# A recurrent layer's products and recurrence, in another order

## Chip, core and metric

The kernel runs on one core of a Trainium2 chip. The metric is the time of one execution on the device in microseconds (us). PE is TensorE, DVE is VectorE, ACT is ScalarE, POOL is GpSimd, SP is SyncE, which issues the loads of weights.

## What is computed

Four layers over 512 tokens of width 1024, all in float32: dilated attention with a SwiGLU FFN, forgetting attention with a SwiGLU FFN and a last norm, then a second block of a gated recurrent mixer and a retention mixer, each between an input norm and an output norm. The change is in the recurrent mixer:

```python
u = h @ w_in                                  # 1024 -> 2 x 1536
xb, gate = u[..., :D_RNN], u[..., D_RNN:]
xb = causal_depthwise_conv(xb, conv_w, conv_b)         # 4 taps
xblk = xb.reshape(bsz, s, 16, 96)
r = sigmoid(einsum('bsnc,ncd->bsnd', xblk, w_a) + b_a)
i = sigmoid(einsum('bsnc,ncd->bsnd', xblk, w_x) + b_x)
log_a = -8.0 * r * softplus(-lam)
a = exp(log_a)
bt = sqrt(-expm1(2.0 * log_a)) * (i * xb)
hseq = associative_scan over tokens: h[t] = a[t] * h[t-1] + bt[t]
y = hseq * silu(gate)
return y @ w_out                              # 1536 -> 1024
```

Its input is the first block's output: the last norm of the first block and the input norm of the mixer are folded into one.

## The kernel before

Activations lie with the feature in the partition and the 512 tokens along the row: a tile is 128 x 512. The residual R has 8 such tiles, a projection's input is a pair XH, XL (a value rounded to fp32r, and what is left of it), and each product is three matmuls: high by high, high by low, low by high. Weights come in units of 128 x 1024 (512 KB) in the order of the program through a ring of 5 slots (RING). SP loads unit u when unit u - 5 is used; ACT makes WH of it (L1053), DVE makes WL (L1561). On both, `split(end)` does this for all units up to `end`, where it stands in the engine's program. A unit of a projection is 24 matmuls of 512 columns (L525): two k by four output tiles by three. PSUM has 8 banks; a group of 4 units fills four of them.

Every engine runs its program in order, with semaphores between them. The order is written out by hand.

Ahead of the recurrent layer stands the second FFN's down projection (D1, 22 units). Its second half ends with four additions to R (`add_out`, L1595), and behind them stand ACT's eight XH (L1251) and DVE's eight XL (L1969). POOL sums squares of R in two ways (L1513 to L1520, `two_norms` on PE multiplies the sums by ones) for the folded norms. DVE then makes the factor RB in three steps (`rb_var`, L1975 to L1979), ACT its root, DVE the reciprocal.

The layer (U["L"], 24 units): three times a group of 4 units for the convolution's input (banks 0 to 3) and a group of 4 for the gate (banks 4 to 7). After a first group DVE scales four tiles into L_XR (L2021), ACT makes the last tap (L1268), DVE the three others (L2008), ACT the high part CH (L1272), DVE the low part CL (L2013). After a second group DVE scales four tiles into L_G (L2032), ACT takes their sigmoid (L1279), POOL multiplies (L1523). Behind the first group DVE also runs `after_first_inputs`: R is scaled with the last norm of the first block (L1985, L1989), and `softplus` of lam in 18 small steps.

Then the block products (U["LG"], 8 units, L961 to L963): for each of four blocks of 3 tiles, one unit for r and one for i, 21 matmuls each. A block's round behind them: six sigmoids (ACT, L1295), exp and tanh (ACT, L1307, L1312), CH + CL, i * x and a * a (POOL, L1532, L1536, L1538), the energy (DVE, L2059), its root (ACT, L1300), i times it (DVE, L2040), three scans (DVE, L2043), the product with the gate (DVE, L2047), high and low of the outputs into CH and CL (ACT L1319, DVE L2053). The products of block j wait for the sigmoids of block j - 1, and those of blocks 2 and up stand on ACT behind the outputs of block j - 2. Last the output projection (U["LO"], 12 units: two groups of 6), sums of squares (L976), and the output norm.

## Time and profile before

| | us |
|---|---|
| median of three runs | 2365.08 (2364.07 to 2365.3) |
| the profiled execution | 2365.22 |
| its span, first to last instruction | 2363.4 |
| PE busy in the span | 2238.7 (95%) |
| DVE, ACT, POOL busy | 1225.6, 798.2, 536.0 |

Times of rows are microseconds from the span's start. A timeline row gives start, busy time, engine, line, operation and tiles; in brackets the idle time before it and what ended that. Rows with x3 hold three instructions. Matmuls overlap, so a row's 0.39 is longer than the distance of two starts.

### The profile page before, as it was taken

The page shows a single profiled execution, that of the slowest core. Times are in us where ns is not written, and L with a number is a line of the kernel's source. Part 1 is how long each engine was busy: PE and PEld are TensorE (multiplying, and loading weights), DVE is VectorE, ACT ScalarE, POOL GpSimd, SP SyncE. Part 2 cuts the span into 40 slices and gives each one's busy share as a digit, 9 for nine tenths or more (in the row PEclk, how much of TensorE's full clock was granted, in tenths as well). Part 3 has the DMA queues.
Part 4 walks back from the last instruction along what each step waited for, and adds up shares of the span by engine and source line. Part 5 has one row for each costly group of instructions (what it writes and reads, how often), then busy time and mean ns, then how long its engine had stood idle before and what let it go on. Part 6 is the DMA issues. An engine that isn't in the chain of part 4 may idle for free.

```text
span 2363.4 us, 26705 instructions
## 1 busy us (share of the span) xinstructions
PE 2238.7 (95%) x10598; PEld 1797.5 (76%) x10598; DVE 1225.6 (52%) x1987; ACT 798.2 (34%) x1334; POOL 536.0 (23%) x355
## 2 busy tenths in 40 slices
PE   7999999998999999999999999998994879999997
PEld 6788886886788888876668888887773757877876
DVE  4666456565644433455457444326848665443342
ACT  3334332443332222233434222213346423323321
POOL 2443234140501101223324011034025131100100
PEclk9999999999999999999999999999997999999999
DMA  4222221221233333332213333332321213222322
GB/s 140 81 68 76 81 81 58 68 72 54 81 98 98 96 94 97 98 99 81 72 63 98 96 93 96 99 98 74 96 89 54 72 59 97 85 76 76 93 77 72
DMA packets 84155, 198.27 MB, mean 84 GB/s; under 512 B 7216, under 2 KB 44208, under 8 KB 84032
## 3 DMA queue, kind: packets, MB, share of 16 engines
q1 hardware_dynamic: 81408, 189.62, 26.2%
q10 hardware_dynamic: 2624, 6.93, 0.9%
q8 instruction: 86, 1.41, 0.3%
q14 instruction: 37, 0.30, 0.0%
HBM read 194.40 MB, written 2.13 MB: 83 GB/s over the span
## 4 chain that ended last, share of the span: by engine, by line
PE 85%; DVE 9%; ACT 3%; issue 2%; DMA 0%; POOL 0%; DVEq 0%; SPq 0%; ACTq 0%
PE PS L525 50%; PE PS L569 5%; PE PS L571 5%; PE PS L570 5%; PE PS L594 2%; PE PS L595 2%; PE PS L596 2%; PE PS L1018 1%; PE PS L642 1%; PE PS L652 1%; PE PS L666 1%; DVE WL L1561 1%; PE PS L897 1%; PE PS L887 1%; ACT WH L1053 1%
## 5 line engine op out<-in xcount | busy, mean ns | idle before, releaser
L1561 DVE TENSOR_TENSOR WL<-WR,WH 128x1024 fp32r<-128x1024 f32 x353 | 478.3, 1365 | 759.0 <-ACT WH L1053 758.3
L1053 ACT ACTIVATE WH<-WR 128x1024 fp32r<-128x1024 f32 x353 | 369.6, 1056 | 709.8 <-DMA WR<-in_ws 700.5
L525 PE MATMUL PS<-XH,WH 128*128 128x512 f32 x1024 | 404.8, 395 | 20.4 <-ACT XH L1062 12.0
L525 PE MATMUL PS<-XH,WL 128*128 128x512 f32 x1024 | 401.5, 392 | 0.0
L525 PE MATMUL PS<-XL,WH 128*128 128x512 f32 x1024 | 401.3, 392 | 0.0
L525 PEld LDWEIGHTS PS<-XH,WH 128*128 128x128 f32 x1024 | 194.1, 190 | 66.1 <-issue 21.1
L569 PE MATMUL PS<-XH,WH 128*128 128x512 f32 x544 | 225.1, 414 | 5.4 <-DVE WL L1561 3.6
L525 PEld LDWEIGHTS PS<-XL,WH 128*128 128x128 f32 x1024 | 194.1, 190 | 41.1 <-issue 1.2
L525 PEld LDWEIGHTS PS<-XH,WL 128*128 128x128 f32 x1024 | 193.9, 189 | 40.9
L571 PE MATMUL PS<-XH,WL 128*128 128x512 f32 x544 | 215.8, 397 | 0.0
L570 PE MATMUL PS<-XL,WH 128*128 128x512 f32 x544 | 215.1, 395 | 0.0
L1451 POOL TENSOR_TENSOR A_SH<-A_SH,A_SIN 128x512 f32<-128x512 f32 x48 | 82.5, 1720 | 270.8 <-DVE A_SH L1746 270.8
L1473 POOL TENSOR_TENSOR F_U<-F_G,F_U 128x1024 f32<-128x1024 f32 x22 | 52.7, 2394 | 400.0 <-DVE F_G L1826 400.0
L525 PE MATMUL PS<-HH,WL 128*128 128x512 f32 x352 | 137.0, 389 | 0.0
L525 PE MATMUL PS<-HL,WH 128*128 128x512 f32 x352 | 137.0, 389 | 0.0
L525 PE MATMUL PS<-HH,WH 128*128 128x512 f32 x352 | 137.0, 389 | 0.0
L569 PEld LDWEIGHTS PS<-XH,WH 128*128 128x128 f32 x544 | 104.5, 192 | 28.1 <-issue 5.0
L1083 ACT ACTIVATE A_P<-A_P,A_ST 128x128 f32<-128x128 f32 (+1 forms) x192 | 79.7, 417 | 131.9 <-DVE A_ST L1689 131.9
L571 PEld LDWEIGHTS PS<-XH,WL 128*128 128x128 f32 x544 | 103.9, 191 | 23.5
L570 PEld LDWEIGHTS PS<-XL,WH 128*128 128x128 f32 x544 | 104.6, 192 | 19.1
L525 PE MATMUL PS<-WH,XH 128*128 128x512 f32 x256 | 99.7, 390 | 0.0
L525 PE MATMUL PS<-WL,XH 128*128 128x512 f32 x256 | 99.7, 389 | 0.0
(332 smaller groups left out, 3763.1 us busy)
## 6 DMA issues: line engine op xcount, KB each, us to landing
WR<-in_ws SPq DMA_DIRECT2D x281, 512.0 KB, 3.6
WR<-in_ws SPq DMA_DIRECT2D x144, 256.0 KB, 3.1
B_CB<-gates ACTq DMA_DIRECT2D x8, 512.0 KB, 3.9
XTOK<-in_x SPq DMA_DIRECT2D x2, 1024.0 KB, 8.4
out<-OUT SPq DMA_DIRECT2D x4, 512.0 KB, 2.6
R_D<-in_decay ACTq DMA_DIRECT2D x4, 256.0 KB, 2.6
GAIN<-in_post ACTq DMA_DIRECT2D x1, 512.0 KB, 5.0
CST<-in_cst SPq DMA_DIRECT2D x1, 320.0 KB, 3.3
```

The costliest lines, as they stand in the source:

```text
L525: mm = pe.matmul(PS[:, bank + o, :], l, r, start=first and kk == 0 and i == 0, stop=last and kk == 1 and i == 2)
L569: pe.matmul(PS[:, bank + o, :], WH[:, s, cols], hi[:, k, :], start=first, stop=False)
L570: pe.matmul(PS[:, bank + o, :], WH[:, s, cols], lo[:, k, :], start=False, stop=False)
L571: return pe.matmul(PS[:, bank + o, :], WL[:, s, cols], hi[:, k, :], start=False, stop=last)
L594: pe.matmul(PS[:, o, :], xh, wh, start=first and kk == 0, stop=False)
L595: pe.matmul(PS[:, o, :], xh, wl, start=False, stop=False)
L596: mm = pe.matmul(PS[:, o, :], xl, wh, start=False, stop=last and kk == 1)
L1053: nc.scalar.activation(WH[:, s, :], WR[:, s, :], ACT.Copy).then_inc(hi_ready, 1)
L1083: x = nc.scalar.activation(A_P[:, n % 2, h, w], A_P[:, n % 2, h, w], ACT.Exp, bias=stat(m, 0, 2 * pair + h, qb), accum_out=stat(m, 1, 2 * ...
L1451: nc.gpsimd.tensor_tensor(A_SH[:, r % 2, :], A_SH[:, r % 2, :], A_SIN[:, :], ALU.mult).then_inc(rot_m, 1)
L1473: nc.gpsimd.tensor_tensor(F_U[:, :, :], F_G[:, :, :], F_U[:, :, :], ALU.mult).then_inc(ht_ready, 1)
L1561: tt(WL[:, s, :], WR[:, s, :], WH[:, s, :].bitcast(F32), ALU.subtract).then_inc(lo_ready, 1)
```

## The change

The weights' order in the layer is a table now, L_ORDER: all 12 units of the convolution's input first, then block 0, the first gate group, block 1, half of the second gate group, block 2, its other half, block 3, the third gate group. PE follows it. The convolution's buffers L_XR and L_XC hold four tiles, L_G holds four tiles instead of twelve, so the gate product and the outputs go in fours (`out_inputs`, `out_sigmoids`, `out_gates`, `outputs`). Block products use banks 4 to 7 in rotation: the first tile of each group is given back earlier, and from the fifth tile on (q = 4) a product waits for a sigmoid of the same block. The groups of the output projection change banks. The new helpers hold the same operations as the loops before: `last_tap` and `conv_high` (ACT) and `convolve` and `conv_low` (DVE) for a convolution tile; `gate_sigmoids`, `decays` (exp and tanh), `energy_root`, and `recurrent_high` (ACT), `energy`, `recur` (product and three scans), `outputs` and `outputs_lows` (DVE), and `recur` on POOL (CH + CL, i * x, a * a) for a block's round. On ACT the last four convolution tiles are begun with L_XR of the third group, so they and all before them stand ahead of the first `gate_sigmoids`. `softplus` stands after the second four convolution tiles. The scaling of R moves behind the recurrence (`first_output`), and the four first XL lows into the down projection's second half.

```diff
+        L_ORDER = [("x", j, i) for j in range(3) for i in range(4)] + [("gates", 0, i) for i in range(2)]
+        L_ORDER += [("g", 0, i) for i in range(4)] + [("gates", 1, i) for i in range(2)]
+        L_ORDER += [("g", 1, i) for i in range(2)] + [("gates", 2, i) for i in range(2)]
+        L_ORDER += [("g", 1, i) for i in range(2, 4)] + [("gates", 3, i) for i in range(2)]
+        L_ORDER += [("g", 2, i) for i in range(4)]
...
-            for j in range(3):
-                if j:
-                    pe.wait_ge(xr_ready, 4 * j)
-                group(U["L"] + 8 * j, 4, XH, XL, 0, ready=x_ready(6),
-                      between=None if j else {3: two_norms})
-                pe.wait_ge(rb_var, 6)
-                if j:
-                    pe.wait_ge(lg_ready, 4 * j)
-                group(U["L"] + 8 * j + 4, 4, XH, XL, 4)
-            pe.wait_ge(xr_ready, 12)
-            pe.wait_ge(lg_ready, 12)
-            for j in range(4):
+            def first_product(j):
+                def free(o):
+                    if j == 1 and o == 2:
+                        pe.wait_ge(rb_var, 6)
+                    if j == 2 and o == 0:
+                        pe.wait_ge(xr_ready, 4)
+                group(at_l("x", j, 0), 4, XH, XL, 4 * (j % 2), ready=None if j else x_ready(6),
+                      between=None if j else {3: two_norms}, free=free)
+            def gate_product(j, a, b):
+                if a == 0:
+                    if j:
+                        pe.wait_ge(lg_ready, 4 * j)
+                    else:
+                        pe.wait_ge(xr_ready, 12)
+                for i in range(a, b):
+                    unit(at_l("g", j, i), i, XH, XL, 0, i == 0, i == 3, True)
+            def block_products(j):
                 pe.wait_ge(ch_ready, 3 * j + 3)
                 pe.wait_ge(cl_ready, 3 * j + 3)
+                if j:
+                    pe.wait_ge(sig_done, 6 * j)
+                else:
+                    pe.wait_ge(xr_ready, 8)
                 for which in range(2):
-                    u = U["LG"] + 2 * j + which
+                    u = at_l("gates", j, which)
                     s = u % RING
                     pe.wait_ge(lo_ready, u + 1)
-                    if j:
-                        pe.wait_ge(sig_done, 6 * (j - 1) + 3 * which + 3)
                     for o in range(3):
+                        q = 3 * which + o
+                        if q >= 4:
+                            pe.wait_ge(sig_done, 6 * j + q - 3)
                         blocks = [(n, i) for n, (i, oo) in enumerate(GATE_BLOCKS) if oo == o]
                         for n, i in blocks:
                             cols = slice(n * P, (n + 1) * P)
-                            b = PS[:, 4 * which + o, :]
+                            b = PS[:, 4 + q % 4, :]
                             pe.matmul(b, WH[:, s, cols], CH[:, 3 * j + i, :], start=n == blocks[0][0], stop=False)
                             pe.matmul(b, WH[:, s, cols], CL[:, 3 * j + i, :], start=False, stop=False)
                             mm = pe.matmul(b, WL[:, s, cols], CH[:, 3 * j + i, :], start=False,
                                            stop=n == blocks[-1][0])
-                    mm.then_inc(unit_used, 1)
+                        mm.then_inc(unit_used if o == 2 else gate_done, 1)
+            for j in range(3):
+                first_product(j)
+            block_products(0)
+            gate_product(0, 0, 4)
+            block_products(1)
+            gate_product(1, 0, 2)
+            block_products(2)
+            gate_product(1, 2, 4)
+            block_products(3)
+            gate_product(2, 0, 4)
             pe.wait_ge(sig_done, 24)
...
-            group(U["LO"], 6, CH, CL, 0, ready=recurrent)
-            group(U["LO"] + 6, 6, CH, CL, 4, between={3: lambda: post_sums(0, 4)})
+            group(U["LO"], 6, CH, CL, 4, ready=recurrent)
+            pe.wait_ge(lg_ready, 12)
+            group(U["LO"] + 6, 6, CH, CL, 0, between={3: lambda: post_sums(0, 4)})
...
-            split(U["D1"] + 26)
             act.wait_ge(gv_ready, 2)
             for k in range(DT):
+                if k == 4:
+                    split(U["D1"] + 26)
...
+                last_tap(4 * j)
+                last_tap(4 * j + 1)
                 for o in range(4):
...
+                    split(u + min(4 * j + 9 + o, 18))
+                    conv_high(4 * j + o)
+                    if o < 2:
+                        last_tap(4 * j + 2 + o)
+            gate_sigmoids(0)
+            decays(0)
+            split(u + 19)
+            energy_root(0)
+            split(u + 21)
+            out_sigmoids(0)
+            split(u + 22)
+            gate_sigmoids(1)
+            split(u + 24)
+            decays(1)
+            split(u + 25)
+            energy_root(1)
+            split(u + 26)
+            gate_sigmoids(2)
+            split(u + 28)
+            decays(2)
+            split(u + 29)
+            recurrent_high(0)
+            out_sigmoids(1)
+            split(u + 30)
+            energy_root(2)
+            gate_sigmoids(3)
+            split(u + 31)
+            decays(3)
+            split(u + 32)
+            recurrent_high(1)
+            split(u + 33)
+            energy_root(3)
+            split(u + 36)
+            out_sigmoids(2)
+            recurrent_high(2)
...
-                    act.wait_ge(y_done, 4)
+                    act.wait_ge(cl_ready, 2 * LT)
                 for k in range(4 * d, 4 * d + 4):
-                    nc.scalar.activation(L_G[:, k, :], PS[:, k, :], ACT.Square).then_inc(post_sq, 1)
+                    nc.scalar.activation(L_SQ[:, k, :], PS[:, (k + 4) % 8, :], ACT.Square).then_inc(post_sq, 1)
...
+            recur(0)
+            out_gates(0)
+            recur(1)
+            recur(2)
+            out_gates(1)
+            recur(3)
+            out_gates(2)
...
+            def folded_low(k):
+                dve.wait_ge(x_hi, 48 + k + 1)
+                dve.wait_ge(r_done, 32 + k + 1)
+                stt(XL[:, k, :], R[:, k, :], GV[:, 1, k:k + 1], XH[:, k, :].bitcast(F32), ALU.mult, ALU.subtract)\
+                    .then_inc(x_lo, 1)
+            for d in range(2):
+                split(dn + (26 if d else 15))
+                dve.wait_ge(unit_used, dn + 11 * (d + 1))
+                for k in range(4 * d, 4 * d + 4):
+                    r_inc(tt(R[:, k, :], R[:, k, :], PS[:, k, :], ALU.add))
+                    if k % 4:
+                        folded_low(k - 1)
+                folded_low(4 * d + 3)
...
-            for k in range(DT):
-                dve.wait_ge(x_hi, 48 + k + 1)
-                stt(XL[:, k, :], R[:, k, :], GV[:, 1, k:k + 1], XH[:, k, :].bitcast(F32), ALU.mult, ALU.subtract)\
-                    .then_inc(x_lo, 1)
...
+            def out_inputs(j):
+                dve.wait_ge(unit_used, at_l("g", j, 3) + 1)
+                if j:
+                    dve.wait_ge(y_done, j)
+                for o in range(4):
+                    tt(L_G[:, o, :], PS[:, o, :], RB[:, 0:T], ALU.mult).then_inc(lg_ready, 1)
...
+                first_inputs(j)
                 for o in range(4):
...
+                    convolve(c)
+                    split(u + min(9 + c, 18))
...
+                if j == 1:
+                    dve.wait_ge(ls_exp, 1)
+                    softplus()
+            energy(0)
+            split(u + 20)
+            recur(0)
+            split(u + 21)
+            out_inputs(0)
+            split(u + 24)
+            energy(1)
+            split(u + 25)
+            recur(1)
+            split(u + 26)
+            outputs(0)
+            split(u + 28)
+            out_inputs(1)
+            split(u + 29)
+            outputs_lows(0)
+            energy(2)
+            split(u + 30)
+            recur(2)
+            split(u + 31)
+            outputs(1)
+            split(u + 32)
+            outputs_lows(1)
+            energy(3)
+            split(u + 34)
+            recur(3)
+            split(u + 36)
+            out_inputs(2)
+            outputs(2)
+            outputs_lows(2)
+            first_output()
```

ACT's program between the convolution and the first decays. L_XC is the convolution's sum, CH its high part, WH a unit's high part, L_G the gate, L_SG its sigmoid, L_R and L_I the two sigmoids of a block. Before:

```order
L1268 ACTIVATE L_XC<-L_XR,VC 128x512
L1272 ACTIVATE CH<-L_XC 128x512
L1053 ACTIVATE WH<-WR 128x1024 x4
L1279 ACTIVATE L_SG<-L_G 128x512 x4
L1295 ACTIVATE L_R<-PS,VC 128x512 x3
L1295 ACTIVATE L_I<-PS,VC 128x512 x3
L1053 ACTIVATE WH<-WR 128x1024 x2
L1307 ACT_TABLE_LOAD
L1307 ACTIVATE L_A<-L_R,L_S 128x512 x3
L1312 ACTIVATE L_R<-L_R,L_S 128x512 x3
L1295 ACT_TABLE_LOAD
L1295 ACTIVATE L_RB<-PS,VC 128x512 x3
```

and now:

```order
L1308 ACTIVATE L_XC<-L_XR,VC 128x512 x2
L1095 ACTIVATE WH<-WR 128x1024
L1315 ACTIVATE CH<-L_XC 128x512
L1308 ACTIVATE L_XC<-L_XR,VC 128x512
L1095 ACTIVATE WH<-WR 128x1024
L1315 ACTIVATE CH<-L_XC 128x512
L1308 ACTIVATE L_XC<-L_XR,VC 128x512
L1315 ACTIVATE CH<-L_XC 128x512 x2
L1331 ACT_TABLE_LOAD
L1331 ACTIVATE L_R_117<-PS,VC 128x512 x3
L1331 ACTIVATE L_I_118<-PS,VC 128x512 x3
L1341 ACT_TABLE_LOAD
```

Between the last convolution tile and the sigmoids of block 0 stood four units and a gate group; now the sigmoids follow at once, and units are split between the convolution's tiles.

ACT around the last block. Before, from the outputs of block 1 (L1319) to the decays of block 3:

```order
L1319 ACTIVATE CH<-L_AB 128x512 x3
L1295 ACT_TABLE_LOAD
L1295 ACTIVATE L_RB<-PS,VC 128x512 x3
L1295 ACTIVATE L_IB<-PS,VC 128x512 x3
L1053 ACTIVATE WH<-WR 128x1024 x2
L1300 ACT_TABLE_LOAD
```

and now, from the first four outputs (L1365) to the sigmoids of block 3 (L1331):

```order
L1365 ACTIVATE CH<-L_W 128x512 x4
L1359 ACT_TABLE_LOAD
L1359 ACTIVATE L_SG<-L_G 128x512 x4
L1095 ACTIVATE WH<-WR 128x1024
L1351 ACT_TABLE_LOAD
L1351 ACTIVATE L_W<-L_W 128x1536
L1331 ACT_TABLE_LOAD
L1331 ACTIVATE L_R_122<-PS,VC 128x512 x3
L1331 ACTIVATE L_I_123<-PS,VC 128x512 x3
```

The gate's sigmoids and the root of block 2 now stand ahead of the sigmoids of block 3.

DVE around the scaling of R (L1989 before, L2091 now; WL is a unit's low part). Before, between the last low of the first convolution group and the small steps of softplus:

```order
L2013 TENSOR_TENSOR CL<-L_XC,CH 128x512
L1561 TENSOR_TENSOR WL<-WR,WH 128x1024 x4
L1985 RECIPROCAL L_X<-L_X 128x512
L1989 SCALAR_TENSOR_TENSOR R<-R,VC,L_X 128x512 x8
L1864 TENSOR_SCALAR L_S<-L_S 128x12
```

and now, behind the recurrence, ahead of the output projection's units from the fifth on:

```order
L1654 TENSOR_TENSOR WL<-WR,WH 128x1024 x2
L2133 TENSOR_TENSOR L_G<-PS,RB 128x512 x4
L2157 TENSOR_TENSOR L_W<-L_H,L_G 128x2048
L2163 TENSOR_TENSOR CL<-L_W,CH 128x512 x4
L2087 RECIPROCAL L_X<-L_X 128x512
L2091 SCALAR_TENSOR_TENSOR R<-R,VC,L_X 128x512 x8
L1654 TENSOR_TENSOR WL<-WR,WH 128x1024 x6
```

The reciprocal and the eight products moved behind 24 more units' low parts, and six of the projection's units stand behind them.

## Rows read from the trace of the kernel before

**Rows 1.** The page: PE's busy time, and the weights' loads (KB, us to landing).

```profile
PE 2238.7 (95%) x10598; PEld 1797.5 (76%) x10598; DVE 1225.6 (52%) x1987; ACT 798.2 (34%) x1334; POOL 536.0 (23%) x355
...
WR<-in_ws SPq DMA_DIRECT2D x281, 512.0 KB, 3.6
```

**Rows 2.** Timeline of PE from the down projection's end to the output projection.

```profile
1610.81 0.77 PE L525 MATMUL PS<-XH,WH 128*128 128x512 f32 x1 [4.11 <-DVE XL L1969]
...
1636.34 1.02 PE L935 MATMUL PS<-L_X,CST 128*128 128x512 f32 x2
...
1639.54 0.50 PE L525 MATMUL PS<-XH,WH 128*128 128x512 f32 x1 [2.19 <-DVE RB L1979]
...
1757.11 0.77 PE L961 MATMUL PS<-CH,WH 128*128 128x512 f32 x1 [4.01 <-issue]
...
1780.63 0.77 PE L961 MATMUL PS<-CH,WH 128*128 128x512 f32 x1 [2.81 <-ACT L_RB L1295]
...
1806.81 0.77 PE L961 MATMUL PS<-CH,WH 128*128 128x512 f32 x1 [14.82 <-ACT L_R L1295]
...
1833.52 0.80 PE L525 MATMUL PS<-CH,WH 128*128 128x512 f32 x1 [14.79 <-ACT L_IB L1295]
...
1862.88 0.80 PE L525 MATMUL PS<-CH,WH 128*128 128x512 f32 x1 [4.94 <-DVE WL L1561]
```

**Rows 3.** Chain of waits in the output projection: start, us, what.

```profile
1897.24 3.43 PE PS L976 x8
1900.67 10.91 PE PS L525 x48
```

**Rows 4.** One stretch: us, busy of PE, PEld, DVE, ACT, POOL, PEclk, DMA, GB/s.

```profile
1806.80:1811.20 4.40, 4.39 (x10) 3.46 (x11) 1.82 (x1) 4.38 (x6) 2.65 (x1) 0.50 0.00 0
```

**Rows 5.** Timeline of POOL: norm sums, gate products, recurrence.

```profile
1630.47 2.28 POOL L1520 TENSOR_TENSOR L_X<-L_X 128x512 f32<-128x512 f32 x1
...
1680.17 5.11 POOL L1523 TENSOR_TENSOR L_G<-L_G,L_SG 128x512 f32<-128x512 f32 x4 [47.42 <-ACT L_SG L1279]
...
1790.25 3.28 POOL L1538 TENSOR_TENSOR L_EB<-L_AB 128x1536 f32<-128x1536 f32 x1 [3.21 <-ACT L_AB L1307]
1793.49 4.33 POOL L1532 TENSOR_TENSOR L_X<-CH,CL 128x1536 f32<-128x1536 f32 x1
```

**Rows 6.** Timeline of DVE in the recurrent layer.

```profile
1649.54 2.46 DVE L2008 SCALAR_TENSOR_TENSOR L_XC<-L_XR,VC,L_XC 128x512 f32<-128x512 f32 x3
...
1652.69 0.69 DVE L2013 TENSOR_TENSOR CL<-L_XC,CH 128x512 fp32r<-128x512 f32 x1 [0.70 <-ACT CH L1272]
...
1666.42 3.35 DVE L1985 RECIPROCAL L_X<-L_X 128x512 f32<-128x512 f32 x1
...
1669.80 5.39 DVE L1989 SCALAR_TENSOR_TENSOR R<-R,VC,L_X 128x512 f32<-128x512 f32 x8
...
1678.74 2.48 DVE L2032 TENSOR_TENSOR L_G<-PS,RB 128x512 f32<-128x512 f32 x4
...
1749.98 4.63 DVE L1561 TENSOR_TENSOR WL<-WR,WH 128x1024 fp32r<-128x1024 f32 x4 [0.26 <-ACT WH L1053]
...
1790.96 9.06 DVE L2043 TENSOR_TENSOR_SCAN L_R<-L_A,L_I 128x512 f32<-128x512 f32 x3
...
1829.38 1.75 DVE L2059 SCALAR_TENSOR_TENSOR L_E<-L_E,L_R 128x1536 f32<-128x1536 f32 x1
...
1856.44 3.46 DVE L2043 TENSOR_TENSOR_SCAN L_RB<-L_AB,L_IB 128x512 f32<-128x512 f32 x3
```

**Rows 7.** Timeline of ACT: table load, sigmoids, root, the output norm's root.

```profile
1777.34 1.28 ACT L1295 ACT_TABLE_LOAD   x1
1778.64 1.84 ACT L1295 ACTIVATE L_RB<-PS,VC 128x512 f32<-128x512 f32 x3
...
1785.42 1.49 ACT L1300 ACTIVATE L_E<-L_E 128x1536 f32<-128x1536 f32 x1
...
1916.78 0.63 ACT L1067 ACTIVATE RB<-RB 128x512 f32<-128x512 f32 x1 [3.11 <-DVE RB L1578]
```

264 lines of the change are left out of this document (126 added, 138 removed).

## The prediction

> **What bounds the kernel now.** I read the page's engine line first: PE (TensorE) is busy for 95% of the span, so only its idle places and its slow clock can be won back [rows 1]. Then PE's timeline through the recurrent layer, where the change is, with the idle time and its releaser in brackets [rows 2]. From the last matmul of the second FFN's down projection (1610.81 less 4.11, so 1606.7 us) to the end of the last L525 matmul of the layer's output projection at 1911.6 [rows 3] are 304.9 us. The work there is 24 + 12 units of 24 matmuls and 8 block units of 21: 1032 matmuls at 0.2273 us (10.91 for 48) are 234.6 [rows 3], and the two norm products and four first sums take 5.3 [rows 2, 3]. Some 65 us are left: 47.7 are the seven idle times of [rows 2], the rest is slow clock and small gaps. After an idle time the granted clock is 0.50, the lower of its two levels (1.2 GHz), for some 4 to 5 us (4.4 in the stretch shown) [rows 4]; a matmul then takes 0.43, so each restart costs some 2 us. The two waits of 14.8 us say what bounds the stretch: PE has only block products left and stands until ScalarE's sigmoids, which stand behind the recurrence chain VectorE, ScalarE, GpSimd. One such round is 26.7 us (1806.81 to 1833.52).
>
> Three prices run through the sum. A VectorE op with its inputs in SBUF and a GpSimd op keep each other waiting: three scans take 3.46 alone and 9.06 beside two GpSimd ops, whose ends at 1793.53 and 1797.82 fit the scans' [rows 5, 6]. A change of function set on ScalarE is 1.28, and the next set's first op starts 0.02 behind it [rows 7]. A unit's low half (WL) takes 1.15 (4.63 for four) [rows 6], after landing in 3.6 [rows 1].
>
> **The change, part by part.** I walk the changed order from 1606.7, engine by engine, with these durations.
>
> *Start.* The lows of XL for k 0 to 3 move into the down projection's second half, beside 11 units of 5.45 us in each of which VectorE makes one WL of 1.15, and PE begins at 1606.7 instead of 1610.8. Four units take 21.8: 1628.5. But the norm products wait for GpSimd's sums, which ended at 1632.75 and start from the same residual tiles as before [rows 5]; with four XL ops fewer beside them I take 1631.0. So of 4.1 plus its slow restart only some 4 remain. The norms take 1.9, VectorE's three steps to rb_var 2.2 as before [rows 2] with six matmuls of the next group ahead of the wait. Then 186 matmuls, 42.3: first_product(2) ends at 1677.4.
>
> *Block 0.* PE goes on for 27 matmuls, 6.1. The fourth tile of six (q = 4) reuses bank 4 and waits for the first sigmoid, which on ScalarE stands behind all twelve convolution tiles; the last four of these begin only when first_product(2) has ended. From 1677.4: a WL's rest and two lows, 1.7; softplus, 3.6 (1678.74 less the end of L1989); four L_XR, 2.5 (as the four L_G); four tiles of taps at 2.46, 9.8; two WL, 2.3; two lows, 1.3; CH 0.6; table load 1.28; a sigmoid 0.6 (1.84 for three) [rows 6, 7]. Together 23.7: 1701.0. PE stands 17.5, **a new stall** that replaces the 4.0, 2.8 and one of the 14.8. After it 15 matmuls, 3.4, and 2.4 for slow clock: 1706.8.
>
> *Middle.* Four g units 21.8, block 1 9.5, two g units 10.9, block 2 9.5 and 0.6 of wait, two g units 10.9: 1770.0. Here the g products hide the recurrence: a round's chain of 20 to 27 us lies beside 20.5 to 31 us of matmuls, where before it lay beside 9.5.
>
> *Block 3.* PE needs its sigmoid at 1776.1. On ScalarE sqrt of block 2 stands ahead, on VectorE out_inputs(1) ahead of that, and this waits for the g unit that ends at 1770.0. Chain: 2.8 because the WL of two units stand behind GpSimd's ops of 3.3 us and more; L_G 2.5; WL 1.15; four lows of outputs beside GpSimd's four L_G products (5.11 for four), 4.9; energy for three tiles 1.75; sqrt 1.5; table load 1.3; sigmoid 0.6: 16.5 [rows 5 to 7], so 1786.5, a wait of 10.4. Then 3.4 and 2.4: 1792.3. The last g product, 21.8: 1814.1.
>
> *Output projection.* Its first four units run to 1835.9. The low of the fifth is on VectorE behind first_output, which the change moves there: reciprocal 3.35 and eight R 5.4 [rows 6]. VectorE gets there late: from 1792.3 GpSimd's three ops of a block (3.4 each, 10.2, between 3.28 and the 4.33 of one held up, and 2.4 lost to VectorE's) to 1804.9; WL, four lows and energy 5.4; sqrt and two WH 2.5, with a wait, 3.6 in all; product and three scans 5.2; two WL 2.3; four L_G 2.5; GpSimd's four products from the first sigmoid on, to 1827.8; product 2.3; high and lows 3.1; first_output 8.8; WL 1.15: 1843.1. PE waits 7.2. Then eight units 43.6, first sums 3.4, slow clock 2.4: **1892.5**. first_output was free before, since it ran in the projection's shadow; here it is the whole of this stall.
>
> *Behind it* nothing changes in kind: squares, sums and the output norm are the same ops in other banks. ScalarE needs one more table load before the root, and it waits 3.11 there for rb_var, so the 1.28 is hidden [rows 7]; without that cover it would cost 1.28.
>
> Sum: 1892.5 against 1911.6, a gain of 19.1. The profiled execution took 2365.22 (span 2363.4), within 0.15 of the median; that gives **2346**.
>
> *Table loads, row and rule.* The row shows 1.28 and no gap after it [rows 7]. The Trainium skill, "ScalarE: Activation LUTs", What ACT_TABLE_LOAD costs, gives 2.66 us for each switch, 1.38 of it a drain. By it three switches on PE's path (blocks 0, 3 and the last sigmoids) would make an estimate 4 us later, 2350. The trace does not show the drain.
>
> *The port, row and rule.* By [rows 5, 6] GpSimd and VectorE wait for each other, but not wholly: part of each GpSimd op runs beside. The Trainium skill, "SBUF — State Buffer", SBUF: two separate sides, calls it an exclusive lock for the whole instruction. By that rule each of the pairs above costs some 0.4 more, about 2 us in all, 2348.
>
> **Rivals.**
> 1. *The port costs less.* If in the new order the pairs miss each other (scans at 3.46 as in the fourth block before), the 2.8 and 2.4 in block 3, 2.4 in the next chain and 1 at the start go, and with them half of what the four lows lose, about 10: 2336. For it: ops without a partner run at the solo price in [rows 6]. Against: the order puts GpSimd's L_G products beside the output lows.
> 2. *More waits at the blocks.* Chains through three in-order queues tend to lose a little at each link. If block 2 waits as block 3 does (10.4 less 0.6) and restarts slow (2.4), 12 are lost: 2358; if it waits half as long, 2352. Against: ScalarE's work ahead of block 2's sigmoid is done 0.6 after PE needs it, by the same prices.
> 3. *Slower.* The g products do not hide the rounds: each block's round of 26.7 starts only when the g product before it is done, because out_inputs(j), the WL of the next units and the sigmoids stand in line behind it on VectorE and ScalarE. For it: before, each round did run alone [rows 2]; against: then PE had nothing else to do. Then from 1706.8: three rounds, 80.1, and 65.4 of g products, 1852.3; projection and its waits 78.4: 1930.7, 19.1 later than before: 2384. It decides at overlap: my forecast has 38 of the 65.4 hidden, and below 19 the change is a loss.
> 4. *Block 0's stall is shorter*, if VectorE is not behind with softplus: 3.6 less, 2342; inside the range.
>
> **How the numbers follow.** The walk as it stands 0.62 (2341 to 2351); rival 1 0.15; rival 2 0.16; rival 3 0.04; rival 4 0.03. The range 2336 to 2356 leaves out the end of rival 1, the far end of rival 2 and rival 3. A difference of 0.2% (5 us) is about what a measurement of this kernel can tell. Faster by more 0.93 (all but the far end of rival 2 and rival 3), same 0.03, slower 0.04.
>
> **What would show it.** In PE's timeline after: no wait at the first unit, one of 2 to 4 us before the norm products; one of 17 in block 0 released by a sigmoid; one of 5 to 12 in block 3; one of 3 to 9 at the fifth unit of the output projection, released by WL; the first output matmul at 1814, the last at 1892. The prediction is wrong if block 1 or 2 waits by more than 3 us, if scans take 9 as a rule, or if the norm's tail grows.

## The result and the profile after

| | before | after |
|---|---|---|
| median, us | 2365.19 (2364.07 to 2365.59, four runs) | 2348.28 (2346.45 to 2349.87, four runs) |
| profiled execution, its span | 2365.22, 2363.4 | 2346.45, 2344.7 |
| end of D1 (last down projection matmul) to end of the output projection | 304.9 | 288.9 |
| from there to the end of the span | 451.8 | 451.8 |

After is 0.9929 of before, with a 95% interval of 0.9913 to 0.9945: 16.9 us less. The forecast walked from D1's end on and gave 19.1 less; from there 16.0 were measured. The time of 2348.28 is 2.3 above the forecast and inside its range.

Both spans are cut at D1's end because PE's program ahead of it is the same and still ends at different times: 1606.7 before, 1603.9 after, and between 1603.7 and 1608.2 in the profiled executions below. D1 itself takes 119.8 in every one of them, whether the four XL lows stand in its second half or not, so the difference arises ahead of it. Whoever compares two single spans puts up to 4.6 us of that down to the change.

The page of after, first section. It answers [rows 1]:

```profile
PE 2230.0 (95%) x10598; PEld 1790.5 (76%) x10598; DVE 1214.4 (52%) x1986; ACT 802.6 (34%) x1337; POOL 544.3 (23%) x355
```

PE is busy 8.7 us less with as many matmuls, as these count longer at the lower clock (5.8 of it between D1's end and the output projection's, 255.2 against 249.4), and its share is 95% in both: this line says little of where the gain is. PE's timeline can. These are all its idle times over 1 us from D1's end to the output projection's end, and the one behind (start, us, what, and in brackets the idle time and its releaser). They answer [rows 2]:

```profile
1629.53 1.49 PE L950 MATMUL PS<-SQS,CST 128*128 128x512 f32 x2 [3.85 <-POOL L_X L1605]
...
1700.57 0.80 PE L992 MATMUL PS<-CH,WH 128*128 128x512 f32 x1 [17.09 <-ACT L_R L1331]
...
1755.92 0.50 PE L992 MATMUL PS<-CH,WH 128*128 128x512 f32 x1 [1.20 <-ACT L_R L1331]
...
1786.12 0.80 PE L992 MATMUL PS<-CH,WH 128*128 128x512 f32 x1 [9.50 <-ACT L_R L1331]
...
1842.94 0.79 PE L541 MATMUL PS<-CH,WH 128*128 128x512 f32 x1 [7.50 <-DVE WL L1654]
...
1906.48 0.77 PE L541 MATMUL PS<-XH,WH 128*128 128x512 f32 x1 [9.20 <-ACT XH L1104]
```

Before, there were eight over 1 us, 49.0 in all: the seven of [rows 2] and this one:

```profile
1686.50 0.47 PE L525 MATMUL PS<-XH,WH 128*128 128x512 f32 x1 [1.30 <-DVE WL L1561]
```

Now they are 39.1 in five. So 9.9 of the 16.0 are idle time, and nearly all the rest is the 5.8 of matmuls at the lower clock. The wait at the layer's first unit is gone, so are both of 14.8. 17.09 is new, and the 4.94 at the fifth unit of the output projection has become 7.50. The chain of waits says what bounds the start (start, us, what); here is its end:

```profile
1624.97 2.06 POOL L_X L1600
1627.03 1.22 POOL SQS L1603
1628.25 1.23 POOL L_X L1605
1629.53 1.49 PE PS L950 x2
1631.01 1.72 PE PS L951 x2
```

From 1606.05 to 1629.5 the chain runs on GpSimd, while PE works beside it. Two stretches of the clock (us, busy of PE, PEld, DVE, ACT, POOL, PEclk, DMA, GB/s), the norm products and the restart in block 0, as in [rows 4]:

```profile
1629.50:1632.70 3.20, 3.17 (x5) 1.39 (x6) 0.00 (x0) 0.00 (x0) 0.00 (x0) 0.60 0.00 0
1700.50:1704.90 4.40, 4.33 (x10) 3.50 (x11) 0.00 (x0) 1.83 (x5) 0.00 (x0) 0.50 0.00 0
```

### The profile page after: what moved, and what is told of

It is laid out like the page before. It is cut to its first block, busy times and chain, and to the rows that moved or that the text cites. A ratio compares the mean times of both kernels' runs of the same rounds, so it can differ in the third digit from the quotient of the medians.

```text
span 2344.7 us, 26703 instructions
## 1 busy us (share of the span) xinstructions
PE 2230.0 (95%) x10598; PEld 1790.5 (76%) x10598; DVE 1214.4 (52%) x1986; ACT 802.6 (34%) x1337; POOL 544.3 (23%) x355
## 3 DMA queue, kind: packets, MB, share of 16 engines
q1 hardware_dynamic: 81408, 189.62, 25.6%
## 4 chain that ended last, share of the span: by engine, by line
PE 85%; DVE 8%; issue 2%; ACT 2%; POOL 2%; DMA 1%; DVEq 0%; SPq 0%; POOLq 0%; ACTq 0%
PE PS L541 50%; PE PS L585 5%; PE PS L587 5%; PE PS L586 5%; PE PS L610 2%; PE PS L611 2%; PE PS L612 2%; PE PS L1060 2%; PE PS L658 1%; PE PS L668 1%; PE PS L682 1%; PE PS L913 1%; PE PS L903 1%; DVE WL L1654 1%; ACT WH L1095 1%
## 5 line engine op out<-in xcount | busy, mean ns | idle before, releaser
L541 PE MATMUL PS<-XH,WH 128*128 128x512 f32 x1024 | 403.1, 394 | 13.0 <-ACT XH L1104 12.7
L586 PEld LDWEIGHTS PS<-XL,WH 128*128 128x128 f32 x544 | 103.7, 191 | 19.1
L541 PE MATMUL PS<-WH,XL 128*128 128x512 f32 x256 | 99.6, 389 | 0.0
```

The lines of the kernel that those rows point to most:

```text
L541: mm = pe.matmul(PS[:, bank + o, :], l, r, start=first and kk == 0 and i == 0, stop=last and kk == 1 and i == 2)
L586: pe.matmul(PS[:, bank + o, :], WH[:, s, cols], lo[:, k, :], start=False, stop=False)
```

## The experiments

All were run against the kernel before; the comparison with after goes through that. The intervals are 2 to 4 us to either side, so a difference of less than some 5 us between two medians is not resolved by them. "Rest" is the span less the end of D1 in the profiled execution (740.7 in after, 756.7 before). It leaves out the part ahead of D1's end, but there is one for each kernel. How well it repeats can be seen where the order is the same: from D1's end to the restart in block 0 is 96.7 to 97.4 in five kernels (after, e_first_early, e_pool_short, e_energy_first, e_g_not_split). Smaller differences below go by the rest and by the waits.

| run | median | of before (95%) | rest |
|---|---|---|---|
| e_first_early | 2338.99 | 0.9888 (0.9873 to 0.9903) | 730.4 |
| e_pool_short | 2343.61 | 0.9908 (0.9895 to 0.9922) | 737.1 |
| e_energy_first | 2345.56 | 0.9919 (0.9905 to 0.9933) | 737.5 |
| e_lows_late | 2351.94 | 0.9943 (0.9931 to 0.9956) | 741.9 |
| e_norm_short | 2341.35 | 0.9899 (0.9882 to 0.9915) | 734.3 |
| e_g_not_split | 2359.84 | 0.9979 (0.9971 to 0.9988) | 752.3 |
| e_sig0_early | 2346.18 | 0.9921 (0.9908 to 0.9933) | 737.3 |
| e_block0_chain | 2341.86 | 0.9902 (0.9888 to 0.9915) | 735.1 |
| e_all | 2335.09 | 0.9873 (0.9860 to 0.9887) | 727.4 |
| e_all_pool_order | 2332.53 | 0.9860 (0.9845 to 0.9875) | 725.3 |
| e_best | 2329.69 | 0.9849 (0.9834 to 0.9863) | 719.6 |
| e_best2 | 2327.60 | 0.9839 (0.9826 to 0.9853) | 719.7 |

### Does first_output make the last wait?

```diff
+            first_output()
             energy(0)
...
             outputs_lows(2)
-            first_output()
```

> The changed kernel with one move: first_output (one reciprocal and eight scaled R tiles on VectorE) stands just before the energy of block 0, in VectorE's idle 17.39 us there, and no longer between the output lows and the low half of the projection's fifth unit. Theory A (first_output is the whole of that stall): the wait of 7.50 at the fifth unit of the output projection goes, and with it some 2 us of slow clock: 8 to 10 us less than the changed kernel's 2348.3, so 2338 to 2341; PE's waits in blocks 0, 2 and 3 stay at 17, 1 and 9.5. Rival B (something else is about as late): the low half then waits for the output highs and lows, for its landing or for WH, and only 0 to 4 us are gained, 2344 to 2348. Rival C: the R tiles beside GpSimd's first ops of block 0 hold those up, and block 2's wait grows by what GpSimd loses, 3 us or more.

Theory A: 9.3 less in the medians, 10.3 in the rest. PE has no idle time over 0.3 us in the output projection, and those in blocks 0, 2 and 3 are 17.30, 1.19 and 9.50. Its last two R tiles lie beside GpSimd's first ops now, and VectorE pays most for it (timeline of VectorE, then of GpSimd, in this run):

```profile
1706.10 11.91 DVE L2091 SCALAR_TENSOR_TENSOR R<-R,VC,L_X 128x512 f32<-128x512 f32 x8
1720.73 1.76 DVE L2140 SCALAR_TENSOR_TENSOR L_W<-L_W,L_R 128x1536 f32<-128x1536 f32 x1 [2.72 <-POOL L_W L1624]
```

```profile
1713.61 3.85 POOL L1621 TENSOR_TENSOR L_I<-L_I,L_W 128x1536 f32<-128x1536 f32 x1
1717.54 3.08 POOL L1624 TENSOR_TENSOR L_W<-L_A 128x1536 f32<-128x1536 f32 x1
```

11.91 instead of 5.39 [rows 6], all of it in the last two tiles (4.01 and 4.00, where the six ahead took 0.75 each), while GpSimd's op took 3.85 for 3.52 in after, and VectorE still waits 2.72 for GpSimd behind them. Rivals B and C fall.

### What makes block 3's wait?

Two runs: GpSimd's products of the second group shortened, and, with nothing left out, another order on VectorE.

```diff
-                    nc.gpsimd.tensor_tensor(L_G[:, o, :], L_G[:, o, :], L_SG[:, o, :], ALU.mult).then_inc(lgs_ready, 1)
+                    n = 1 if j == 1 else T
+                    nc.gpsimd.tensor_tensor(L_G[:, o, 0:n], L_G[:, o, 0:n], L_SG[:, o, 0:n], ALU.mult).then_inc(lgs_ready, 1)
```

> The changed kernel in which GpSimd's four L_G products of the second output group cover 1 of 512 columns (the rest of that group's gate product is left out). They lie beside VectorE's four output lows (6.81 us, against 2.49 alone) ahead of block 3's sigmoid. Theory A (block 3's wait is made by these pairs): the lows take 2.5, the energy, the root and the sigmoid come 4 to 4.5 earlier, PE's wait in block 3 falls from 9.50 to 5 to 5.5, and the time by 4 to 5: 2343 to 2344.5. Rival B (the lows are not on that chain, or the root's table load and WH stand there anyway): block 3's wait stays above 8 and the time within 1 of 2348.3. Rival C (later waits take it back): block 3's wait falls but the one at the projection's fifth unit grows, gain under 2.

```diff
-            outputs_lows(0)
             energy(2)
+            outputs_lows(0)
```

> The changed kernel with two steps swapped on VectorE: the energy of block 2 ahead of the four output lows of the first group, not behind them; nothing is left out. Theory A (in the run with GpSimd's L_G products cut to one column PE's wait in block 3 fell from 9.50 to 5.18, so what counts there is the 6.81 us of lows beside them): the energy starts some 6 to 7 earlier, takes 2 to 4 beside GpSimd, and the root follows: PE's wait in block 3 falls to 3.5 to 5.5, 4 to 6 us less than 2348.3: 2342 to 2344.5. Rival B (the energy itself is held up by GpSimd's products, or the lows now hold up VectorE's product and scans and so outputs of group 1): block 3's wait falls but a later wait grows, gain under 2.

The rows of after first: VectorE's four lows, GpSimd's products beside them.

```profile
1774.07 6.81 DVE L2163 TENSOR_TENSOR CL<-L_W,CH 128x512 fp32r<-128x512 f32 x4
1780.80 1.74 DVE L2140 SCALAR_TENSOR_TENSOR L_W<-L_W,L_R 128x1536 f32<-128x1536 f32 x1
```

```profile
1773.00 7.33 POOL L1610 TENSOR_TENSOR L_G<-L_G,L_SG 128x512 f32<-128x512 f32 x4
```

Shortened, they leave the lows alone (VectorE's timeline in e_pool_short):

```profile
1775.42 2.49 DVE L2164 TENSOR_TENSOR CL<-L_W,CH 128x512 fp32r<-128x512 f32 x4
```

and PE a wait of 5.18 instead of 9.50: 4.3 less, 4.7 in the medians, 3.7 in the rest, and the wait at the fifth unit stays at 7.49: theory A, and rivals B and C fall. The new order brings it down further, to 3.88, but 2.62 come up behind it. PE's timeline in e_energy_first, and VectorE's:

```profile
1783.92 0.79 PE L992 MATMUL PS<-CH,WH 128*128 128x512 f32 x1 [3.88 <-ACT L_R L1331]
...
1802.52 0.50 PE L541 MATMUL PS<-XH,WH 128*128 128x512 f32 x1 [2.62 <-DVE WL L1654]
```

```profile
1788.82 10.02 DVE L2149 TENSOR_TENSOR_SCAN L_H<-L_A,L_I 128x512 f32<-128x512 f32 x3
1798.76 3.70 DVE L1654 TENSOR_TENSOR WL<-WR,WH 128x1024 fp32r<-128x1024 f32 x1
```

The scans (3.46 in after) now meet GpSimd's ops of block 3 and take 10.02, with a low half behind them. The wait at the fifth unit falls to 5.79. In sum 2.7 less in the medians and 3.3 in the rest, where A wanted 4 to 6 and B under 2: block 3's wait fell as A said, and a later one took part of it back, as B said.

### What is the start worth?

```diff
-                    if k % 4:
-                        folded_low(k - 1)
-                folded_low(4 * d + 3)
...
+            for k in range(DT):
+                folded_low(k)
```

> The changed kernel with the lows of XL after all eight R adds of the down projection again, as in the kernel before; all else as changed. Theory A (the start is bound by GpSimd's norm sums, so folding the lows is worth little): PE waits some 4 us at the first unit and restarts slowly, but no longer waits before the norm products (3.85 now), which run at full clock: 0.5 to 2.5 us slower than 2348.3, so 2349 to 2351. Rival B (the fold is worth its whole wait): 4 to 6 us slower, 2352 to 2354. Rival C (the sums are slowed by the folded lows as much as these save): the same or up to 2 us faster, 2346 to 2348.

```diff
+                w = 1 if k == 7 else T
-                nc.gpsimd.tensor_tensor(first[:, :], R[:, k, :], R[:, k, :], ALU.mult).then_inc(sq_mul, 1)
+                nc.gpsimd.tensor_tensor(first[:, 0:w], R[:, k, 0:w], R[:, k, 0:w], ALU.mult).then_inc(sq_mul, 1)
```

(and `w` columns in the three steps behind it; the rest of the last tile's part of both sums is left out)

> The changed kernel in which GpSimd's four steps of the norm sums for the last residual tile cover 1 of 512 columns (the rest of that tile's part of both sums is left out). They took 5.6 us, and PE waited 3.85 for the last of them before the norm products. Theory A (the start of the layer is bound by GpSimd's sums, and all that follows hangs on it): no wait before the norm products, which then run at full clock and no longer take 3; every later wait of PE stays as it was; 4.5 to 6.5 us less than 2348.3: 2342 to 2344. Rival B (the next link, from VectorE's steps on the norm to the convolutions, is as late): the wait in block 0 grows by what the start gains; within 2 of 2348.3.

With the lows late PE waits 3.96 at the first unit and not at all before the norms; the restart in block 0 is 98.8 after D1's end instead of 96.7, and 1.2 of that is left in the rest. The medians say 3.7, between theories A and B, and the intervals overlap; the waits and the rest say A, that most of the fold is not gained, since GpSimd's sums come next. The other run shows the other side. PE's timeline in e_norm_short:

```profile
1628.24 1.02 PE L950 MATMUL PS<-SQS,CST 128*128 128x512 f32 x2
1629.10 1.02 PE L951 MATMUL PS<-L_X,CST 128*128 128x512 f32 x2
1629.56 0.79 PE L541 MATMUL PS<-XH,WH 128*128 128x512 f32 x1
...
1698.19 0.80 PE L992 MATMUL PS<-CH,WH 128*128 128x512 f32 x1 [17.31 <-ACT L_R L1331]
```

No wait, 1.32 from the first norm product to the next unit's first matmul (2.20 in after, from 1629.53 to 1631.73), and all behind it 5 us earlier, with the same wait in block 0. 6.9 less in the medians, 6.5 in the rest: theory A, a little above its 4.5 to 6.5. GpSimd's sums were worth more than their wait of 3.85.

### Do the g units hide the rounds?

```diff
-        L_ORDER += [("g", 1, i) for i in range(2)] + [("gates", 2, i) for i in range(2)]
-        L_ORDER += [("g", 1, i) for i in range(2, 4)] + [("gates", 3, i) for i in range(2)]
+        L_ORDER += [("gates", 2, i) for i in range(2)]
+        L_ORDER += [("g", 1, i) for i in range(4)] + [("gates", 3, i) for i in range(2)]
...
-            gate_product(1, 0, 2)
             block_products(2)
-            gate_product(1, 2, 4)
+            gate_product(1, 0, 4)
```

> The changed kernel in which the second gate group of the projection is not split: all four of its units (21.8 us of PE) stand between block 2 and block 3, none between block 1 and block 2. The work is the same. Theory A (a round of the recurrence costs PE what of it is not beside g units): block 2 loses 10.9 of cover, and its wait goes from 1.20 to 10 to 13; block 3's sigmoid waits for the L_G of units that now end some 11 to 13 later, so its wait stays at 8 to 10: 10 to 14 slower than 2348.3, 2358 to 2362. Rival B (the rounds are paced by their own chain, 27 to 30 from sigmoid to sigmoid, wherever the g units stand): block 2 waits 10 more and block 3 10 less, and the time stays within 3 of 2348.3.

PE's timeline:

```profile
1759.27 0.79 PE L992 MATMUL PS<-CH,WH 128*128 128x512 f32 x1 [10.76 <-ACT L_R L1330]
...
1801.13 0.79 PE L992 MATMUL PS<-CH,WH 128*128 128x512 f32 x1 [8.62 <-ACT L_R L1330]
```

Block 2 waits 10.76 instead of 1.20, block 3 8.62 instead of 9.50, and the time grows by 11.6 (and as much in the rest): theory A. With the same work, two units taken from between the rounds cost their own 10.9.

### Is block 0's wait ScalarE's order?

```diff
                     split(u + min(4 * j + 9 + o, 18))
+                    if j == 2 and o == 0:
+                        gate_sigmoids(0, 0, 4)
                     conv_high(4 * j + o)
...
+                    if j == 2 and o == 1:
+                        gate_sigmoids(0, 4, 6)
-            gate_sigmoids(0)
```

> The changed kernel with one move on ScalarE: the first four sigmoids of block 0 stand behind the first low of the third group of convolutions is due (after its first two last taps), the last two after its last tap, no longer all six behind the twelfth convolution tile. Theory A (block 0's 17 us are ScalarE's order alone): the first sigmoid starts at about 13 us earlier, PE's wait in block 0 falls from 17.09 to 3 to 5, ScalarE's decays and so the energy of block 0 come 9 to 12 earlier (VectorE idles there for 5 to 8 rather than 17.39), waits in blocks 2 and 3 grow by 0 to 4 together: 8 to 12 us less than 2348.3, so 2336 to 2340. Rival B (the later chain does not follow): GpSimd's first ops now lie beside VectorE's taps and both lose time, and the later blocks' waits grow by most of what block 0 gave: a gain under 4, 2344 to 2349.

My theory fell on its size: 2.1 in the medians, 3.4 in the rest, for 8 to 12. Block 0's wait did fall to 4.40. But (PE's timeline, then VectorE's, then GpSimd's)

```profile
1690.97 0.50 PE L992 MATMUL PS<-CH,WH 128*128 128x512 f32 x1 [4.40 <-ACT L_R L1333]
...
1731.63 0.80 PE L992 MATMUL PS<-CH,WH 128*128 128x512 f32 x1 [6.96 <-ACT L_R L1333]
```

```profile
1696.59 8.75 DVE L2124 SCALAR_TENSOR_TENSOR L_XC<-L_XR,VC,L_XC 128x512 f32<-128x512 f32 x3
...
1715.24 1.76 DVE L2145 SCALAR_TENSOR_TENSOR L_W<-L_W,L_R 128x1536 f32<-128x1536 f32 x1 [5.54 <-POOL L_W L1629]
```

```profile
1696.40 3.62 POOL L1622 TENSOR_TENSOR L_W<-CH,CL 128x1536 f32<-128x1536 f32 x1 [63.80 <-PE PS L994]
1700.10 3.83 POOL L1626 TENSOR_TENSOR L_I<-L_I,L_W 128x1536 f32<-128x1536 f32 x1
```

The early sigmoids and products let GpSimd start 13 us sooner, beside VectorE's taps, and these took 8.75 instead of 2.46. ScalarE's decays still stood behind the last convolution tile, and this came late by that. So the energy came 4.5 earlier, not 9 to 12 (from D1's end), and block 1, which had not waited, waited 6.96 for a sigmoid that stands behind `out_sigmoids(0)`. The next run moves `decays(0)` behind the last of the early sigmoids, and `gate_sigmoids(1)` ahead of `out_sigmoids(0)`:

```diff
                     if j == 2 and o == 1:
                         gate_sigmoids(0, 4, 6)
+                        decays(0)
-            decays(0)
...
+            gate_sigmoids(1)
             out_sigmoids(0)
...
-            gate_sigmoids(1)
```

> The run with block 0's sigmoids moved gained 2.1 where 8 to 12 were expected: its trace shows three taps at 8.75 beside GpSimd's first two ops (2.46 alone), decays only after the last convolution tile, and PE waiting 6.96 in block 1 for a sigmoid that stands behind out_sigmoids. Here, on top of it: block 0's exps and tanhs follow its sigmoids directly, ahead of the last two high parts, and block 1's sigmoids stand ahead of the first output sigmoids. Theory A (these two places on ScalarE kept the gain): PE's wait in block 1 goes to 0 to 1, VectorE's energy of block 0 starts 4 to 6 earlier than in that run; in all 7 to 12 less than 2348.3, 2336 to 2341. Rival B (what is left is VectorE beside GpSimd): block 2's wait grows to 5 or more and the gain stays at 2 to 5, 2343 to 2346.

Block 1's wait is gone, block 2's is 7.66 (1.20 in after), and 6.4 are gained, 5.6 in the rest: more than rival B's range, less than A's. The energy comes 2.9 earlier than in e_sig0_early, not 4 to 6, as the three taps now lie beside three of GpSimd's ops. Block 2's wait is not B's mechanism alone: VectorE's energy of block 1 waits there 11.13 for GpSimd, whose ops of block 1 stand behind the first gate products. e_all_pool_order changes that order.

### All together

> The moves together on the changed kernel: the block 0 chain, the energy of block 2 ahead of the output lows, and first_output cut in two (the reciprocal and three R tiles after the first L_G, five after the scans of block 2). Theory A (the gains add, since each takes away another of PE's waits): 7 to 12 of block 0, 4 to 6 of block 3, 8 to 10 of the output projection: 19 to 28 less, 2320 to 2329. Rival B (the rounds take the place of the waits): once block 0's and block 3's waits are gone, the chain over VectorE, ScalarE and GpSimd bounds each block again, waits of 3 to 8 come up in blocks 1 to 3, and 10 to 15 are gained, 2333 to 2338.

e_all joins e_block0_chain and e_energy_first, and has `first_output` in two parts: the reciprocal and three R tiles behind `out_inputs(0)`, five R tiles behind the scans of block 2. 13.2 less than after: rival B's size. Waits of 8.84 in block 2, 4.62 in block 3 and 4.55 at a g unit behind it; the last two add up to more than the 3.88 and 2.62 of e_energy_first. On GpSimd (timeline in e_all) the first group's products stand ahead of block 1's ops:

```profile
1725.98 6.41 POOL L1615 TENSOR_TENSOR L_G<-L_G,L_SG 128x512 f32<-128x512 f32 x4 [21.40 <-ACT L_SG L1361]
1732.36 4.50 POOL L1622 TENSOR_TENSOR L_W<-CH,CL 128x1536 f32<-128x1536 f32 x1
```

```diff
             recur(0)
+            recur(1)
             out_gates(0)
-            recur(1)
```

> The run with all moves together, and one more: on GpSimd the recurrence ops of block 1 stand ahead of the first output group's four L_G products, as they already do for block 2. In that run PE waited 8.84 in block 2, and GpSimd's ops of block 1 stood 6.4 behind those products. Theory A (GpSimd's order made that wait): block 2's wait falls to 0 to 2, block 3's stays at 3 to 6; 6 to 9 less than that run's 2335.1: 2326 to 2329. Rival B (VectorE, now beside GpSimd at once, loses what the order gains): block 2's wait stays at 5 or more, 2332 to 2336.

2.6 less than e_all in the medians (the intervals overlap), 2.1 in the rest, where A wanted 6 to 9: block 2's wait is 3.00, with 1.75 for a low half at its start, and the g unit behind block 3 waits 5.69. The wait lies between A and B, the time is B's.

> As the last, with two more moves: ScalarE's sigmoids of block 3 stand ahead of the root of block 2 (one change of function set less on the way to them), and the eight scaled R tiles stand behind the low half of the projection's eighth unit (five) and ninth unit (three), where VectorE idles 4.1 twice; the reciprocal stays behind the first L_G. Theory A: block 3's wait falls to 0 to 2 and the 4.55 behind it, which five R tiles made ahead of a low half, to 0 to 2: 2317 to 2323. Rival B (the chain of block 2's root, product and scans comes later and PE then waits in the last g units or in the output projection for the group's outputs): one wait of 3 to 6 comes up there, 2323 to 2328. Rival C: the R tiles in the projection delay its lows, and PE waits there.

e_best has on ScalarE `gate_sigmoids(3)` ahead of `energy_root(2)`, and the eight R tiles in the output projection (`scaled(0, 5)` behind `split(U["LO"] + 8)`, `scaled(5, 8)` behind `split(U["LO"] + 9)`). The median of 2329.69 is above the ranges of both theories. The output projection has no wait, so rival C falls. Block 3's is 1.77, as A said; but one wait stays, not at 3 to 6 in the last g units, as B said, but at 7.62, at the first g unit behind block 3. PE's timeline in e_best there, and VectorE's ahead of it:

```profile
1784.71 0.79 PE L541 MATMUL PS<-XH,WH 128*128 128x512 f32 x1 [7.62 <-DVE WL L1659]
```

```profile
1769.72 11.24 DVE L2170 TENSOR_TENSOR CL<-L_W,CH 128x512 fp32r<-128x512 f32 x4
1780.89 3.77 DVE L1659 TENSOR_TENSOR WL<-WR,WH 128x1024 fp32r<-128x1024 f32 x1
```

The four lows have become 11.24. The last run puts them behind the scans of block 2:

> As e_best, with the four output lows of the first group on VectorE behind the product and scans of block 2 and the low halves of the next two units (both directly behind the energy and the scans). In e_best these lows took 11.24 beside GpSimd's products and block 3 ops (2.49 alone), and PE waited 7.62 for the low half behind them. Theory A (that order alone made the wait): it goes to 0 to 2, 5 to 8 less than e_best's 2329.7: 2321.5 to 2325. Rival B (whatever VectorE does beside GpSimd's ops is held up by as much, now the scans): the wait moves to the next low half, 3 to 6 there, and the time stays at 2327 to 2330.

The 7.62 went, and 3.58 (at the start of block 3, for a low half), 0.89 (a g unit) and 4.12 (ahead of the output projection) came; the rest is the same, 719.7 against 719.6, and the medians' 2.1 are not resolved. Rival B. Both are faster than before and after: e_best2 is 0.9839 of before, 20.7 us less than after.

## Why the prediction held, point by point

Times from D1's end, forecast and measured in after:

| step | forecast | measured |
|---|---|---|
| norm products start | 24.3 | 25.6 |
| block 0: wait begins, lasts | 76.8, 17.5 | 79.6, 17.09 |
| block 2 waits | 0.6 | 1.20 |
| block 3: wait lasts, ends | 10.4, 179.8 | 9.50, 182.2 |
| fifth unit of the output projection: wait lasts, ends | 7.2, 236.4 | 7.50, 239.0 |
| last output matmul ends | 285.8 | 288.9 |

- **What bounds the stretch.** That g units between the blocks hide the rounds is shown by e_g_not_split; rival 3 (no overlap) is excluded with it.
- **The start is the mis-sized term.** I took GpSimd's sums to end 24.3 after D1, 1.7 earlier than before, with four XL ops fewer beside them. They ended at 25.55 (before: 26.05), so the four XL ops gave back 0.5. The trace of after shows what took their place: a unit's low half on VectorE. Beside one, a step of the sums takes about twice as long (GpSimd's timeline, then VectorE's):

```profile
1619.20 1.04 POOL L1600 TENSOR_TENSOR L_X<-SQT,GV 128x512 f32<-128x512 f32 x1
1620.19 2.27 POOL L1603 TENSOR_TENSOR SQS<-SQS,SQT 128x512 f32<-128x512 f32 x1
1622.43 1.28 POOL L1605 TENSOR_TENSOR L_X<-L_X 128x512 f32<-128x512 f32 x1
```

```profile
1619.34 1.98 DVE L1654 TENSOR_TENSOR WL<-WR,WH 128x1024 fp32r<-128x1024 f32 x1 [3.79 <-ACT WH L1095]
```

  Four such steps took 2.06 to 2.27 where the others of their kind took 1.04 to 1.28. By my estimate from these rows they lose some 4.1 of the 5.6 that the sums lose in all, and the rest goes to the R adds and the lows that stay. Before, three such steps (1.84 to 2.28) lost some 2.8, and the XL ops took 3.1. No run moved the low halves, so this is read and not shown.

  And I priced the norm products at 1.9; behind a wait they ran at a granted clock of 0.60, took 2.2 and left the next unit a slow begin. So PE reached block 0's wait 2.8 late, and that is nearly all of the 3.1 at the end. e_norm_short shows that this term reaches the end undiminished.
- **Block 0's stall**: forecast from the chain of VectorE's convolution tiles and ScalarE's order, 0.4 off. Right in size. That it is ScalarE's order that keeps the sigmoid there is shown too (4.40 in e_sig0_early); rival 4 is not seen.
- **Block 3**: 0.9 off; its pair, lows beside GpSimd's products, is shown by e_pool_short. Here two misses cancel, which is luck. I had priced the lows at 4.9, they took 6.81. And I had put 2.8 on low halves that are not done when the g unit ends; they took 9.00 for two beside GpSimd, but were done 0.06 before its end (1770.43 and 1770.49), so VectorE's next op started at 1770.53.
- **first_output** is the whole of the last stall, as e_first_early shows. Before, the same unit waited 4.94 for its low half [rows 2], so against that kernel this stall is 2.6 more.
- **Behind it** 451.8 in both, and the wait there 9.20 against 9.21: nothing.
- **The slow restarts.** I gave each wait some 2 us of slow clock. Behind 17.09, 9.50 and 7.50 the granted clock is 0.50 for 4.5 us or so; behind the 1.20 of block 2 it is 1.00 (1755.9 to 1760.0).
- **The profiled execution** took 2346.45 where I said 2346. That is luck: 2.8 of its 18.8 less lie ahead of D1's end, where such differences come without the change, and 3.1 were missed behind it.
- **Rival 1** (pairs miss each other) came true for the scans (3.46 four times in after) but not for the lows, nor for low halves and the product (VectorE, in after; [rows 6] gives 4.63 for four low halves):

```profile
1761.43 9.00 DVE L1654 TENSOR_TENSOR WL<-WR,WH 128x1024 fp32r<-128x1024 f32 x2
...
1796.58 5.60 DVE L2157 TENSOR_TENSOR L_W<-L_H,L_G 128x2048 f32<-128x2048 f32 x1
```

 **Rival 2** did not: block 2 waits 1.20.
- **The table load** on ScalarE on the way to block 3's sigmoid, in after:

```profile
1784.08 1.28 ACT L1331 ACT_TABLE_LOAD   x1
1785.38 1.84 ACT L1331 ACTIVATE L_R<-PS,VC 128x512 f32<-128x512 f32 x3
```

The first sigmoid starts 0.02 behind the load, as in [rows 7], and the load starts 0.02 behind the root's end at 1784.06. The 1.38 us of drain in the Trainium skill ("ScalarE: Activation LUTs", What ACT_TABLE_LOAD costs) does not show here either.
- **The port.** I held that part of a GpSimd op runs beside a VectorE op. The three taps of e_sig0_early lay beside GpSimd's two ops, which ended at 1700.02 and 1703.93. VectorE's timeline has these for the first two:

```profile
1696.59 3.98 DVE L2124 SCALAR_TENSOR_TENSOR L_XC<-L_XR,VC,L_XC 128x512 f32<-128x512 f32 x1
...
1700.68 3.80 DVE L2124 SCALAR_TENSOR_TENSOR L_XC<-L_XR,VC,L_XC 128x512 f32<-128x512 f32 x1
```

  Each ended 0.55 behind the end of a GpSimd op, less than the 0.75 that it takes alone, and the third, with no GpSimd op beside it, took 0.75. So of a GpSimd op's 3.6 to 3.8 us hardly any went to a tap. That is close to the rule that I had set against my reading (the Trainium skill, "SBUF — State Buffer", SBUF: two separate sides: the loser blocks for the whole instruction). By the estimate in the prediction the rule was worth some 2 us here; other misses are as large, so the time of after does not decide it.

## What to carry to other kernels

A unit of matmuls that needs nothing from a recurrence is worth its full length as cover between two rounds of it (two such units taken away cost 11.6 us here, their own length being 10.9). It stops being cover where an in-order queue ahead of the next sigmoid gets its input from that same unit, as for block 3 here: with all four units ahead of it (e_g_not_split) PE still waited 8.62.

Once a wait is taken away, the next link of the chain takes part of it back. In e_sig0_early block 0 restarted 12.7 earlier (from D1's end), block 2 only 3.6: two places in ScalarE's order kept some of that (e_block0_chain), GpSimd's order some (e_all_pool_order), and VectorE beside GpSimd some; how much each, these runs do not separate. So before a step is moved on VectorE, look at what GpSimd does beside its new place.

Work that nobody waits for (here the scaling of R) belongs where its engine idles with a low half already made, and not ahead of the one low half that PE needs next.

## What was not expected of the hardware

- VectorE beside GpSimd lost as much as the forecast's scans (9.06 for 3.46) or more: three taps 8.75 (2.46 alone), four lows 11.24 (2.49), three scans 10.02 (3.46), eight R tiles 11.91 (5.39). The rows share a pattern: while GpSimd's ops follow each other, VectorE gets about one op done for each of them, however short its own is. A tap of 0.75 took 3.98 and 3.80, an R tile of 0.75 took 4.01 and 4.00, and a low half of 1.2 took 4.54 twice beside ops of 5.12 and 4.38 in after; but a low of 0.68 took only 1.74 to 1.79 beside gate products of 1.70 to 2.31. So it is the length of GpSimd's op that sets the price, and many short VectorE ops beside long GpSimd ops lose most. e_pool_short agrees: with the gate products cut to one column the lows took 2.49 for four, as alone. The rest of the pattern is read from the traces.

  GpSimd's ops beside the taps took 3.62 and 3.83; alone they take, in after:

```profile
1706.59 3.51 POOL L1617 TENSOR_TENSOR L_W<-CH,CL 128x1536 f32<-128x1536 f32 x1 [77.12 <-PE PS L994]
1710.18 3.52 POOL L1621 TENSOR_TENSOR L_I<-L_I,L_W 128x1536 f32<-128x1536 f32 x1
```

  Elsewhere they lose more: 5.12 for the first of block 2 in after, and four gate products took 10.00 in e_best (5.04 for the last four in after), twice their length, where VectorE's lows took 4.5 times theirs.
- Not every VectorE op is held up. In after four L_G tiles, which read PSUM and one SBUF tile, took 2.48 from 1770.53 on, as alone, though GpSimd's a * a ran until 1773.03:

```profile
1770.53 2.48 DVE L2133 TENSOR_TENSOR L_G<-PS,RB 128x512 f32<-128x512 f32 x4
```

```profile
1769.42 3.61 POOL L1624 TENSOR_TENSOR L_W<-L_A 128x1536 f32<-128x1536 f32 x1
```

- A wait of 3.85 before two short products cost 6.5 us by the time that it was gone (e_norm_short): 5.1 of it had been gained by block 0's restart (91.55 against 96.65 after D1's end); where the other 1.4 lies is not settled. It comes in small parts, 0.75 of it between the restarts of blocks 0 and 2, and this stretch, whose order is the same, took 54.6 to 55.3 in six kernels, so part of it may be chance.
